# Real part of a two-dimensional Fourier transform on half of the channels, with output weights folded on VectorE

## What is computed

```python
def _fourier(f):                      # f (B, T=512, 512): 4 groups of 128 channels
    fg = f.reshape(B, T, F_GROUPS, F_GROUP_DIM).astype(jnp.float32)
    y = jnp.fft.fft2(fg, axes=(1, 3), norm="ortho").real
    return y.reshape(B, T, D_F).astype(f.dtype)

def _merge(p, attn_o, four_o, w_o_attn, w_fourier, w_out):
    ga = jax.nn.sigmoid(p[..., OFF_GA:OFF_GB])
    gb = jax.nn.sigmoid(p[..., OFF_GB:N_IN])
    return (ga * (attn_o @ w_o_attn) + gb * (four_o @ w_fourier)) @ w_out
...
    p = h @ w_in[l]
    q, k, v = _mla_qkv(p, *mla_w, tabs)
    attn_lat = _attend_latent(q, k, v, kc, vc)
    four_lat = _fourier(p[..., OFF_F:OFF_GA])
    x = x + g1 * _merge(p, attn_lat, four_lat, w_o_attn[l], w_fourier[l], w_out[l])
```

## Time and profile before

| | us |
|---|---|
| median of 3 runs | 1301.1 |
| lowest, highest | 1300.31, 1302.43 |
| the profiled execution | 1301.71 |
| its span, first to last instruction | 1299.9 |
| PE busy in it | 1282.9 (99%) |
| DVE busy | 671.2 |
| ACT busy | 473.3 |
| POOL busy | 453.3 |

### The profile page before, as it was taken

One profiled execution on the slowest core, in us unless ns is written; L12 is line 12 of the kernel. 1 busy time (PEld: TensorE's weight loads), 2 busy tenths in 40 slices (PEclk: granted clock), 3 DMA queues, 4 the chain that ended last, 5 costly groups with the idle time before them and its releaser, 6 DMA issues.

```text
span 1299.9 us, 15446 instructions
## 1 busy us (share of the span) xinstructions
PE 1282.9 (99%) x6176; PEld 945.6 (73%) x6176; DVE 671.2 (52%) x1182; ACT 473.3 (36%) x641; POOL 453.3 (35%) x215
## 2 busy tenths in 40 slices
PE   8999999999999999999999999999999999999998
PEld 5789888766687644443457788888888888888887
DVE  2466877768772633432349458322551541551553
ACT  4354232366432221111155651433431431331443
POOL 3144266167540000000043252544354444444440
PEclk9999999999998999999999999999999999999999
DMA  9532288110227899999963121322123123123101
GB/s 377 226 114 93 111 344 339 52 34 33 95 109 299 314 422 422 420 420 421 421 235 126 65 98 66 130 97 98 65 99 128 65 98 130 65 97 129 66 1 65
DMA packets 33907, 227.06 MB, mean 175 GB/s; under 512 B 3888, under 2 KB 4528, under 8 KB 7856
## 3 DMA queue, kind: packets, MB, share of 16 engines
q1 hardware_dynamic: 32256, 218.79, 43.7%
q0 software_dynamic: 1152, 4.19, 0.9%
q10 hardware_dynamic: 432, 3.15, 0.6%
HBM read 221.92 MB, written 4.19 MB: 174 GB/s over the span
## 4 chain that ended last, share of the span: by engine, by line
PE 93%; DMA 4%; DVE 2%; SPq 1%; ACT 0%; issue 0%; DVEq 0%
PE psum L985 24%; PE psum L986 23%; PE psum L987 23%; PE psum L1516 11%; DMA ex_more<-in_stream 2%; PE psum L1287 2%; DMA mod_in<-in_stream 2%; PE psum L1258 1%; PE psum L1601 1%; DVE x L2583 1%; PE psum L1476 1%; PE psum L1501 0%; PE psum L1504 0%; PE psum L1243 0%; PE psum L1029 0%; PE psum L1004 0%
## 5 line engine op out<-in xcount | busy, mean ns | idle before, releaser
L915 POOL TENSOR_TENSOR w_lo<-raw,w_hi 128x1024 fp32r<-128x1024 f32 x79 | 192.0, 2430 | 555.7 <-ACT w_hi L1802 554.3
L985 PE MATMUL psum<-b_hi,w_hi 128*128 128x512 f32 x608 | 238.2, 392 | 0.1
L987 PE MATMUL psum<-b_hi,w_lo 128*128 128x512 f32 x608 | 236.8, 389 | 0.0
L986 PE MATMUL psum<-b_lo,w_hi 128*128 128x512 f32 x608 | 236.7, 389 | 0.0
L1802 ACT ACTIVATE w_hi<-raw 128x2048 fp32r<-128x2048 f32 x80 | 152.6, 1908 | 147.6 <-PE psum L987 99.3
L917 POOL TENSOR_TENSOR w_lo<-raw,w_hi 128x1024 fp32r<-128x1024 f32 x79 | 197.2, 2496 | 0.0
L985 PEld LDWEIGHTS psum<-b_hi,w_hi 128*128 128x128 f32 x608 | 114.2, 188 | 30.7 <-issue 5.7
L987 PEld LDWEIGHTS psum<-b_hi,w_lo 128*128 128x128 f32 x608 | 114.2, 188 | 24.0
L986 PEld LDWEIGHTS psum<-b_lo,w_hi 128*128 128x128 f32 x608 | 114.2, 188 | 23.1
L1516 PE MATMUL psum<-ex_ring,xe 128*64 128x512 f32 x432 | 95.0, 594 | 0.0
L2581 DVE TENSOR_TENSOR x<-psum,x 128x512 f32<-128x512 f32 x39 | 26.9, 691 | 127.7 <-PE psum L987 127.7
(11 more groups left out here) (460 smaller groups left out, 2277.1 us busy)
## 6 DMA issues: line engine op xcount, KB each, us to landing
raw<-in_stream SPq DMA_DIRECT2D x97, 1024.0 KB, 4.8
ex_ring<-in_stream SPq DMA_DIRECT2D x78, 1024.0 KB, 19.9
ex_more<-in_stream SPq DMA_DIRECT2D x18, 1024.0 KB, 21.7
mod_in<-in_stream SPq DMA_DIRECT2D x8, 1024.0 KB, 21.6
x<-in_x SPq DMA_DIRECT2D x4, 512.0 KB, 5.9
x<-in_x ACTq DMA_DIRECT2D x1, 2048.0 KB, 7.6
xt<-h2t SPq DMA_DIRECT2D x8, 256.0 KB, 8.2
out<-y_out SPq DMA_DIRECT2D x4, 512.0 KB, 3.0
```

Of the source, the lines that this page charges most:

```text
L915: nc.gpsimd.tensor_tensor(w_lo[:, slot, w], raw[:, raw_slot, w], w_hi[:, slot, w].bitcast(F32), ALU.subtract)
L985: mm(o, w[0], x[0], start=start, stop=False)
L986: mm(o, w[0], x[1], start=False, stop=False)
L987: return mm(o, w[1], x[0], start=False, stop=stop)
```

## The change

The cosine columns of a real transform are even in the channel and the sine columns odd: outputs c and 128-c share them. The changed kernel forms for each group only channels 0 to 64 of the cosines and 1 to 63 of the sines, and puts the mirrored half into the output weights.

- `dftc` has 128 columns: channel 0 halved, cosines 1 to 63, and then the cosine of channel 64 (in the place of sine 0) and sines 1 to 63. `f_ch` is one tile per group, with products of 128 columns instead of 256.
- Positions: two groups share one stationary operand (64 channels each). For each of two pairs gp, `four_e` (258 columns, even part) and `four_s` (256 columns, odd part); one tile `four_x` for channel 64 of the 4 groups, a stationary operand of 4 columns. DVE forms no halves here; the parts go as they are into `e_hi`/`e_lo`, `o_hi`/`o_lo` and `xs`.
- Output weights: for each j five blocks of 128 (two plain, two mirrored, one for channel 64). They lie in chunks 15 (j = 0, 1), 16 (j = 2, 3, 7) and 18 (j = 4, 5, 6); the keys' and values' blocks move into chunk 17. DVE turns plain and mirrored weights a, b in the raw buffer into a+b and a-b (`fold_four`, two instructions over 2, 3 and 3 times 256 elements per partition), and ACT rounds these chunks only behind it.
- Output: `four_even` (6 products of 258 columns and 2 small ones of 258 columns for channel 64) and `four_odd` (6 products of 256 columns) for each j, into two tiles. ACT copies the odd one to SBUF (`four_copy`), and `four_gate` forms the two halves of the positions in PSUM (2 x 255 columns) before the multiplication of 512.
- Order: `MOD_BEHIND` puts one modulation chunk behind chunk 16 and one behind chunk 17 (two behind 16 before). On DVE gates 0 and 1 now stand between modulation chunks 14 and 15, the folds behind chunks 11 and 13 and between the key sums 2 and 3. Three of the five fills move from DVE to POOL, two to an earlier place. Chunk 18 is rounded by ACT ahead of the square of key tile 3 instead of tile 0. Ahead of head 0, j = 4 and 5 both stand before the transposes, the maxima stand in pairs behind `four_even` and `four_odd` of j = 6 and 7 and use the banks of the transposed keys (3, 4), and PE waits for all gates before head 0's output.

```diff
+FO_PARTS = [(15, 243 * B, (0, 1)), (16, 256 * B, (2, 3, 7)), (18, 288 * B, (4, 5, 6))]
+S1_FO = {j: first + i * 5 * B for _, first, js in FO_PARTS for i, j in enumerate(js)}
+CF = 64
+EW = T // 2 + 2
...
-MOD_BEHIND = {8: 1, 9: 1, 10: 2, 11: 2, 12: 2, 13: 2, 14: 2, 15: 2, 16: 2}
+MOD_BEHIND = {8: 1, 9: 1, 10: 2, 11: 2, 12: 2, 13: 2, 14: 2, 15: 2, 16: 1, 17: 1}
...
+    if c == FO_CHUNKS[2]:
+        due.append(TILE["uk", 3])
...
+    def four_o(j, name, bank=None):
+        p.add(name, j, by=("resid_done", j + 1) if name == "four_o" else "act", split=blocks(s1, S1_FO[j], 5), bank=bank)
...
-    four_o(4, 0)
+    for j, b in ((4, (6, 7)), (5, (0, 1))):
+        four_o(j, "four_o", b[0])
+        four_o(j, "four_d", b[1])
     head_t(0)
-    four_o(5, 1)
-    for j in (6, 7):
-        four_o(j, (2, 0)[j - 6])
-        for i in range(4 * (j - 6), 4 * (j - 5)):
-            p.add("mx", 0, i // 2, i % 2, bank=6 + i % 2)
+    for j, b in ((6, (2, 1)), (7, (7, 6))):
+        four_o(j, "four_o", b[0])
+        max_pair(0, 2 * (j - 6))
+        four_o(j, "four_d", b[1])
+        max_pair(0, 2 * (j - 6) + 1)
     head_t(1)
-    p.add("mx_row", 0, by="act", bank=2)
+    p.add("mx_row", 0, by="act", bank=0)
...
+                if c == FO_CHUNKS[2] - 1:
+                    pool.wait_ge(tile_full, TILE["gb", KD - 1] + 1)
+                    pool.wait_ge(w_lo_done, c + 1)
+                    nc.gpsimd.memset(k_hi[0][QK:QK + 1, :].bitcast(F32), 1.0).then_inc(rows_set, 1)
...
-            for g in range(NF + 1):
-                if g < NF:
-                    pe.wait_ge(lo_done, SPLITS["f", g] + 1)
-                    for half in range(2):
-                        o = open_tile("f_ch", g, half)
-                        for t in range(2):
-                            tok = slice((2 * half + t) * P, (2 * half + t + 1) * P)
-                            last = mm3(o[:, t * 256:(t + 1) * 256], (f_hi[:, g, tok], f_lo[:, g, tok]),
-                                       (dftc_hi[:], dftc_lo[:]), True, True)
-                        done(last)
-                if g >= 1:
-                    pe.wait_ge(lo_done, SPLITS["f_ch", g - 1, 1] + 1)
-                    for name, part, first, n in (("four_s", 1, FH, FH), ("four", 0, 0, FH + 2)):
-                        o = open_tile(name, g - 1)
-                        a = slice(part * P, part * P + P)
-                        for t in range(TT):
-                            x_hi, x_lo = weights(s1, S1_DFT + t * T, T)
-                            last = mm3(o[:, 0:n], (fc_hi[:, (g - 1) % 2, t // 2, t % 2, a], fc_lo[:, (g - 1) % 2, t // 2, t % 2, a]),
-                                       (x_hi[:, first:first + n], x_lo[:, first:first + n]), t == 0, t == TT - 1)
-                        done(last)
+            for g in range(NF):
+                pe.wait_ge(lo_done, SPLITS["f", g] + 1)
+                o = open_tile("f_ch", g)
+                for t in range(TT):
+                    tok = slice(t * P, (t + 1) * P)
+                    last = mm3(o[:, t * 2 * CF:(t + 1) * 2 * CF], (f_hi[:, g, tok], f_lo[:, g, tok]),
+                               (dftc_hi[:], dftc_lo[:]), True, True)
+                done(last)
+
+            def positions(name, part, first, n, channels, rows=P):
+
+                o = open_tile(*name)[0:rows, 0:n]
+                for t in range(TT):
+                    x_hi, x_lo = weights(s1, S1_DFT + t * T, T)
+                    last = mm3(o, (channels(fc_hi[:, t, part, :, :]), channels(fc_lo[:, t, part, :, :])),
+                               (x_hi[:, first:first + n], x_lo[:, first:first + n]), t == 0, t == TT - 1)
+                done(last)
+
+            for gp in range(2):
+                pe.wait_ge(lo_done, SPLITS["f_ch", 2 * gp + 1] + 1)
+                pair = lambda x: x[:, 2 * gp:2 * gp + 2, :].rearrange("p g c -> p (g c)")
+                positions(("four_e", gp), 0, 0, EW, pair)
+                positions(("four_s", gp), 1, FH, FH, pair)
+            positions(("four_x",), 1, 0, EW, lambda x: x[:, :, 0], NF)
...
-            def four_out(j, behind=None):
-
-                o = open_tile("four_o", j)
-                for k in range(NF):
-                    last = mm3(o, weights(s1, S1_FO[j] + k * B, B), (f_hi[:, k, :], f_lo[:, k, :]), k == 0, k == NF - 1)
-                    if k == NF - 1:
-                        done(last)
-                    if behind is not None:
-                        behind(k)
+            pe.wait_ge(lo_done, SPLITS["four_x"] + 1)
+
+            def four_even(j):
+
+                o = open_tile("four_o", j)[:, 0:EW]
+                for gp in range(2):
+                    mm3(o, weights(s1, S1_FO[j] + gp * B, B), (e_hi[:, gp, :], e_lo[:, gp, :]), gp == 0, False)
+                x_hi, x_lo = weights(s1, S1_FO[j] + 4 * B, B)
+                mm(o, x_hi[0:32 + NF, :], xs[:], start=False, stop=False)
+                done(mm(o, x_lo[0:NF, :], xs[0:NF, :], start=False, stop=True))
+
+            def four_odd(j):
+
+                o = open_tile("four_d", j)[:, 0:FH]
+                for gp in range(2):
+                    last = mm3(o, weights(s1, S1_FO[j] + (2 + gp) * B, B), (o_hi[:, gp, :], o_lo[:, gp, :]), gp == 0, gp == 1)
+                done(last)
 
             for j in range(KD // 2):
-                four_out(j)
+                four_even(j)
+                four_odd(j)
...
-            four_out(4)
+            for j in (4, 5):
+                four_even(j)
+                four_odd(j)
             head_t(0)
-            four_out(5)
-            four_out(6, lambda k: max_tile(0, k // 2, k % 2))
-            four_out(7, lambda k: max_tile(0, 2 + k // 2, k % 2))
+            for j in (6, 7):
+                four_even(j)
+                max_pair(0, 2 * (j - 6))
+                four_odd(j)
+                max_pair(0, 2 * (j - 6) + 1)
             head_t(1)
             max_row(0)
             def pv_pair(h, k):
 
+                if k == 0 and h == 0:
+                    pe.wait_ge(resid_done, KD)
...
+                    if c in FO_CHUNKS:
+                        act.wait_ge(fo_folded, FO_CHUNKS.index(c) + 1)
...
+            def four_copy(j):
+
+                o = take("four_d", j)
+                if j >= 2:
+                    act.wait_ge(resid_done, j - 1)
+                A(four_d[j % 2][:], o[:, 0:FH], ACT.Copy).then_inc(freed_act, 1)
+
             for j in range(KD // 2):
-                split_weights(TILE["four_o", j])
+                four_copy(j)
...
+            def fold_four(i):
+
+                c, first, js = FO_PARTS[i]
+                n = RAW_OF_SPLIT[FO_CHUNKS[i]]
+                dve.wait_ge(raw_full[n % NRAW], 16 * (n // NRAW + 1))
+                w = raw[:, n % NRAW, first - c * CH:first - c * CH + len(js) * 5 * B].rearrange("p (j b) -> p j b", b=5 * B)
+                a, b = w[:, :, 0:2 * B], w[:, :, 2 * B:4 * B]
+                link(V.tensor_tensor(a, a, b, ALU.add))
+                V.scalar_tensor_tensor(out=b, in0=b, scalar=-2.0, in1=a, op0=ALU.mult, op1=ALU.add).then_inc(fo_folded, 1)
+
+            def four_gate(j):
+
+                o, d = take("four_o", j), four_d[j % 2]
+                dve.wait_ge(freed_act, PLAN.freed_count(TILE["four_d", j]))
+                V.tensor_tensor(o[:, T - 1:FH:-1], o[:, 1:FH], d[:, 1:FH], ALU.subtract)
+                link(V.tensor_tensor(o[:, 1:FH], o[:, 1:FH], d[:, 1:FH], ALU.add))
+                V.tensor_tensor(gbf[:, j, :], o, gbf[:, j, :], ALU.mult).then_inc(resid_done, 1)
+
             for c in range(16):
                 modulation_b(c)
-
-            def four_gate(j):
-
-                o = take("four_o", j)
-                dve.wait_ge(freed_act, PLAN.freed_count(TILE["gb", j]))
-                V.tensor_tensor(gbf[:, j, :], o, gbf[:, j, :], ALU.mult).then_inc(resid_done, 1)
-
-            for j in range(KD // 2):
-                four_gate(j)
-
-            V.memset(k_hi[0][QK:QK + 1, :].bitcast(F32), 1.0)
-            V.memset(k_lo[0][QK:QK + 1, :].bitcast(F32), 0.0)
-            V.memset(q_lo[0][QK:QK + 1, :].bitcast(F32), 0.0)
-            V.memset(k_hi[1][QK:QK + 1, :].bitcast(F32), 1.0)
-            V.memset(k_lo[1][QK:QK + 1, :].bitcast(F32), 0.0).then_inc(v_done, 1)
+                if c == 4:
+                    V.memset(k_hi[1][QK:QK + 1, :].bitcast(F32), 1.0)
+                    V.memset(k_lo[1][QK:QK + 1, :].bitcast(F32), 0.0)
+                if c == 11:
+                    fold_four(0)
+                if c == 13:
+                    fold_four(1)
+                if c == 14:
+                    four_gate(0)
+                    four_gate(1)
+            four_gate(2)
+            four_gate(3)
...
+                if t == 2:
+                    fold_four(2)
...
-    dftc = np.concatenate([np.cos(angc) * norm, np.sin(angc) * norm], axis=1).astype(f)
+    dftc = np.concatenate([np.cos(angc[:, :1]) * (norm / 2), np.cos(angc[:, 1:CF]) * norm, np.cos(angc[:, CF:CF + 1]) * norm,
```

(6 more changed lines are left out.)

121 lines of the change are left out of this document (60 added, 61 removed).

## The result

| | before | after |
|---|---|---|
| median, us | 1300.96 | 1310.16 |
| lowest to highest | 1300.31 to 1302.43 (4 runs) | 1309.51 to 1311.97 (4 runs) |
| ratio, 95% interval | | 1.0069 [1.0057, 1.0081] |
| span of the profiled execution | 1299.9 | 1308.4 |
| mean granted clock of PE | 0.996 | 0.988 |

A forecast was written before the change was run, and what follows sets the result against it. PE was taken to bound nearly everywhere and to save 13.2 us alone, but the DVE, ACT and POOL relay gives back all but 0.3: 1301.7 - 0.3 = 1301.4, less 0.6 to the median, 1300.8 us; range 1295 to 1305.

The forecast's parts named there:

- What bounds the kernel: Whole kernel: PE, busy 99% of the span, bounds it nearly everywhere, as long as what feeds it keeps up.
- PE's gain: Fourier stage and output step: PE alone 13.2 us less, 5.0 from the former and 8.2 from the latter.
- The term of the two small products: Output step, channel 64: products of 36 and 4 rows taken by their columns; bounds -1.9 to +1.7 us over all 16.
- The first wait: PE waiting for chunk 16 after two outputs: 1.1 us, or 3.7 if one more pair of pieces or a fold meets POOL.
- The second wait: PE waiting for chunk 17 behind outputs 2 and 3, ahead of the keys: another 2.3 us.
- how the numbers follow: Weighing of the cases: 1298.5 to 1303.7 us has 0.42; a tenth each below 1295 and above 1305.
- rival 2: Waits around 214 to 224 and sparse PE around 250 to 258 drop the clock: 1303.5 to 1306.5 us, chance 0.29.
- The key rows: DVE's rows behind the key sums: unchanged, ending at 245.9 as before, so PE's gain is gone there.
- Ahead of head 0: Key rows to head 0: DVE bounds; score waits save 3.5 us, gates cost 2.0; first product at 259.9, 0.3 earlier.
- Rival 1: From modulation 12 on, POOL and DVE meet less, chunk 16 comes without a wait: 1294 to 1298 us, chance 0.29.
- Rival 3: Channel step at 0.06 us a product: 2.4 us earlier up to chunk 11, 1299 us; within the forecast's 0.42.
- The prediction's own signs: First query product 111.3, POOL waits up 3 to 5 us, third fold 230 to 232, last key row 245 to 246.5.

The follow-up runs named there:

- e8_nofold_rows: Changed kernel without the three DVE folds and ACT's waits for them, and with 128 rows for channel 64: 1296.8 us, 0.9965 of before.
- e4_nofold: Changed kernel without the three DVE folds and ACT's waits for them (output projection not the reference's): 1297.0 us, 0.9974 of before.
- e3_fill: Changed kernel with 34 additional products that compute nothing where PE waits for chunk 16: 1306.0 us, 1.0036 of before.
- e1_rows: Changed kernel with channel 64's operand zero-filled to 128 rows, so both small output products take 128 rows: 1303.9 us, 1.0019 of before.
- e7_rows_early_fill2: Changed kernel with 128 rows for channel 64, folds of chunks 16 and 18 earlier, 10, 5 and 11 additional products ahead of head 0: 1299.1 us, 0.9980 of before.
- e14_fill_both: Changed kernel with 34 additional products at PE's wait for chunk 16 and 10, 5 and 11 ahead of head 0: 1304.3 us, 1.0023 of before.
- e2_fold1: Changed kernel with the fold of chunk 16 behind modulation chunk 12 instead of 13: 1306.0 us, 1.0032 of before.
- e5_rows_fill: Changed kernel with 128 rows for channel 64 and 46 additional products where PE waits for chunk 16: 1306.4 us, 1.0039 of before.
- e15_all_fills: e7_rows_early_fill2 with 18 additional products where PE waits for chunk 16 as well: 1301.3 us, 0.9994 of before.

## Why the prediction was wrong

- **What bounds the kernel** was right in part. The relay of DVE, ACT and POOL sets when chunk 16 comes, and with the folds gone it sets the end: e8_nofold_rows relieves PE and gains nothing over e4_nofold. In the changed kernel itself PE's pace counted as well: filling its first wait gave 4.1 us (e3_fill), full rows 6.3 us (e1_rows).
- **PE's gain.** The channel step's 0.11 was right (0.112). The move of the first stretch was right: the gates end 5.6 us earlier, against 5.0. The term of the two small products was mis-sized: forecast 0.12 each with 0.23 as the upper end, measured 0.32 and 0.1 for each neighbour, 0.55 us a block, 4.4 us in all. e1_rows shows that it lies in the number of rows. The bounds came from products with 128 rows; the fewest in the rows read was 97.
- **The first wait** was foreseen at its place, 1.1 to 3.7 us, and was 4.3. The fold of chunk 16 ended at 210.5 instead of 207.9, since chunk 11's pieces ended 1.3 us later and the four pieces of 12 and 13 took 9.1 us instead of 8.1; then POOL took 6.6 us instead of 5.7, because DVE's next modulation pieces stood beside both of its halves (3.31 and 3.32 us). The second wait, 2.3 us ahead of the keys, did not come: POOL ended chunk 17 at 224.9, and PE at half clock reached the keys at 227.3.
- **The step that failed is "how the numbers follow".** I let the likeliest case keep the clock at 1.00 through a wait of 1 to 4 us, and gave the fall to rival 2, with 4.5 us lost and 1 hidden and a chance of 0.29. The sum so holds nothing for the clock. It fell behind the unfilled first wait of seven profiled executions, with waits of 5.7, 5.7, 4.3, 3.9, 3.0, 2.3 and 1.7 us; only in e7_rows_early_fill2, with waits of 2.4 and 1.3 us, it did not, so the length of the wait alone does not tell. Its cost is 5.9 us by e14_fill_both, more than the 3.5 of rival 2. That rival had it down for 6 and 3 us; it was down for about 13 and 10, in which a small product took 0.51 us. The range ended at 1305, cut through that rival.
- **The key rows** ("follow unchanged and end at 245.9 as before", "whatever PE saved") were late by 6.9 us: 3.5 from PE's slow blocks at half clock, by e3_fill (2.8 by e14_fill_both), 2.1 from the first instruction of the inverse root beside POOL, and the rest, 1.3 to 2.0, by difference only. It goes with the later chunks 16 and 17 and was not isolated. The 2.1 us are an omission: I followed chunk 18 through ACT and not on to POOL, whose work then lay beside a DVE instruction with two SBUF inputs.
- **Ahead of head 0** I had 14.0 us from key row to first product; it was 16.3, and 12.7 with both waits filled. The account of DVE's work was 1.3 us too long, and the fall of the clock cost the 3.6 us between these two.
- **Rival 1** (the relay keeps up, 1294 to 1298) has the time of e4_nofold, 1297, where POOL ended chunk 16 at 212.8 (forecast there 212.4). But that took removing the folds; with them the relay did not keep up. **Rival 3** did not occur: the channel step's pace was the one forecast.
- **The prediction's own signs.** The first query product started at 110.9 (forecast 111.3) and PE's waits for POOL gained 4.3 us (3 to 5). The third fold came 3 us late (234.8), the last key row ended at 252.8, and the clock under 1.00 between 214 and 262 was named as the sign of being wrong.
- The port rule was cited for the folds only. The runs show it at three places: modulation pieces (3.35 to 3.42 us for 1.27), the fold of e2_fold1 (2.95 for 0.95) and the small instruction (2.32 for 0.21). The Trainium skill, SBUF — State Buffer, section Terms, describes it as an exclusive lock of the shared port pair; these rows agree.

## What to carry to other kernels

A wait of PE costs more than its length: in the changed kernel the clock stood at half for 13 us from its first wait on and for 10 us around the maxima of head 0. What that costs depends on whether PE is late at the next hand-over (filling the first wait gave back 4 us in e3_fill and nothing in e5_rows_fill). When weights are folded on the engine that already sets the pace of a supply chain, count the folds by when they let the chunk go, not by their duration: 5.2 us of folds cost 13 here, the fall of the clock included, and 7 with full rows. Give a small contraction the full 128 rows with zeros rather than the few it needs, and follow every moved step to the end of its chain, to the engine that shares its port.

## What the runs showed of the hardware

- A product of 258 columns with 36 or 4 of 128 rows starts 0.32 us before its successor and delays the products around it by 0.1 each; with 128 rows it is 0.12. A stationary operand with only 4 columns has the full pace (0.12). In the kernel before, a product of 96 rows and 384 columns between products of 128 rows started 0.18 us before its successor (250.53 to 250.71), so not every number under 128 is slow. Why few rows are slow was not tested.
- The clock fell to 0.50 behind PE's waits of 4.3 us, of 5.7 and even of 1.7 us (e2_fold1), not behind one of 2.4 us (e7_rows_early_fill2), and also where PE was only sparsely busy (2.5 of 4 us, 254 to 258). With products that compute nothing in both places it stayed at 1.00 (e14_fill_both, e15_all_fills).
- A DVE instruction of 48 columns with both inputs in SBUF took 2.32 us, and 0.21 alone; it ended with the POOL subtraction beside it (2.41 us). Reductions with one SBUF input took 0.70 us beside POOL as alone.
